# The cosine half of the index rotation moves behind TensorE's rotation, and its results are announced one by one

## The reference

```python
def rope(t):
    ...
    return jnp.concatenate([t1 * cos - t2 * sin, t1 * sin + t2 * cos], axis=-1)

p_rwkv, p_att, p_idx, p_gate = jnp.split(proj, c, axis=-1)
...
q_idx, k_idx, w_idx = jnp.split(p_idx, ci, axis=-1)
q_idx = rope(q_idx.reshape(B, S, IDX_HEADS, IDX_DIM))   # 8 heads of 64
k_idx = rope(k_idx[:, :, None, :])[:, :, 0, :]          # one key head of 64

# in the attention, for each block of 128 queries:
sc = jax.nn.relu(jnp.einsum('bqhd,bsd->bqhs', qib, k_idx))
score = jnp.einsum('bqhs,bqh->bqs', sc, wib) * idx_scale
_, sel = lax.top_k(score, topk)
```

## Time and profile before

| what | us |
|---|---|
| median of 3 runs | 2181.82 |
| lowest and highest run | 2179.98, 2184.24 |
| the profiled execution, its own time | 2179.98 |
| span of the profiled execution | 2178.2 |
| PE busy in the span | 2041.2 (94%) |
| PEld busy | 1637.1 (75%) |
| DVE busy | 926.5 (43%) |
| ACT busy | 804.3 (37%) |
| POOL busy | 984.4 (45%) |

### The profile page before, as it was taken

How to read it: one execution, slowest core, us unless ns; L and a number is a source line. 1 busy time by engine, 2 the same in 40 slices (tenths; PEclk the granted TensorE clock), 3 DMA queues, 4 the chain that set the end, 5 groups by cost and what they waited for, 6 DMA issues and landing times.

```text
span 2178.2 us, 26374 instructions
## 1 busy us (share of the span) xinstructions
PE 2041.2 (94%) x10214; PEld 1637.1 (75%) x10214; DVE 926.5 (43%) x1510; ACT 804.3 (37%) x1057; POOL 984.4 (45%) x766
## 2 busy tenths in 40 slices
PE   5997899999999998999999788999999899999998
PEld 3685797775777886888888576975886687888886
DVE  2579556666443134222200578347934452121101
ACT  3455224236555233222222453333225643222221
POOL 3535533545112454655466364003433255555663
PEclk9998999999999999999999899999999999999999
DMA  7211105521111231322222311001221222222222
GB/s 290 78 43 55 40 20 222 226 99 58 40 39 59 97 135 59 112 98 97 98 99 98 125 59 59 2 30 62 94 97 59 97 78 97 97 97 97 89 105 77
DMA packets 25898, 194.96 MB, mean 90 GB/s; under 512 B 3120, under 2 KB 3376, under 8 KB 4912
## 3 DMA queue, kind: packets, MB, share of 16 engines
q1 hardware_dynamic: 25776, 193.29, 24.4%
HBM read 189.09 MB, written 4.19 MB: 89 GB/s over the span
## 4 chain that ended last, share of the span: by engine, by line
PE 82%; DVE 8%; ACT 4%; POOL 2%; issue 2%; DMA 1%; SPq 0%; ACTq 0%; DVEq 0%; POOLq 0%
PE ps L399 22%; PE ps L401 22%; PE ps L400 22%; PE ps L467 2%; POOL W L2467 2%; ACT W L1272 1%; DMA ar<-ada_dram 1%; PE ps L497 1%; PE ps L837 1%; DVE ar L1831 1%; DVE ar L1857 1%; PE ps L892 1%; DVE ar L1809 1%; PE ps L824 1%; PE ps L601 1%
## 5 line engine op out<-in xcount | busy, mean ns | idle before, releaser
L2467 POOL TENSOR_TENSOR W<-raw,W 128x512 fp32r<-128x512 f32 x588 | 774.9, 1318 | 987.3 <-ACT W L1272 951.0
L399 PE MATMUL ps<-hH,W 128*128 128x512 f32 x1648 | 660.9, 401 | 46.0 <-DVE xL L1794 8.3
L401 PE MATMUL ps<-hH,W 128*128 128x512 f32 x1648 | 647.0, 393 | 0.0
L400 PE MATMUL ps<-arR,W 128*128 128x512 f32 x1392 | 542.8, 390 | 0.0
L1272 ACT CAST W<-raw 128x2048 fp32r<-128x2048 f32 x147 | 280.9, 1911 | 576.2 <-PE ps L401 551.2
L399 PEld LDWEIGHTS ps<-hH,W 128*128 128x128 f32 x1648 | 313.1, 190 | 130.7 <-issue 53.8
L401 PEld LDWEIGHTS ps<-hH,W 128*128 128x128 f32 x1648 | 312.6, 190 | 67.0
L400 PE MATMUL ps<-xL,W 128*128 128x512 f32 x848 | 335.4, 396 | 0.0
L400 PEld LDWEIGHTS ps<-arR,W 128*128 128x128 f32 x1392 | 262.1, 188 | 54.8 <-issue 0.2
L399 PE MATMUL ps<-arR,W 128*128 128x512 f32 x592 | 231.3, 391 | 3.3 <-DVE ar L1914 3.3
L401 PE MATMUL ps<-arR,W 128*128 128x512 f32 x592 | 231.1, 390 | 0.0
(11 more groups left out here) (384 smaller groups left out, 2264.9 us busy)
## 6 DMA issues: line engine op xcount, KB each, us to landing
raw<-panels_dram SPq DMA_DIRECT2D x147, 1024.0 KB, 4.8
ar<-ada_dram SPq DMA_DIRECT2D x12, 2048.0 KB, 11.4
xT<-xT_dram SPq DMA_DIRECT2D x2, 2048.0 KB, 9.0
out_dram<-xT SPq DMA_DIRECT2D x8, 512.0 KB, 2.6
xT<-out_dram SPq DMA_DIRECT2D x1, 2048.0 KB, 8.2
wide<-wide_dram SPq DMA_DIRECT2D x1, 1024.0 KB, 4.8
cm<-cm_dram SPq DMA_DIRECT2D x1, 832.0 KB, 30.6
ar<-lora_dram SPq DMA_DIRECT2D x1, 512.0 KB, 3.3
```

The source lines that it names most:

```text
L399: mm(out, lhs[0], rhs[0], start=first, stop=False)
L400: mm(out, lhs[0], rhs[1], start=False, stop=False)
L401: return mm(out, lhs[1], rhs[0], start=False, stop=final)
L2467: ins = tt(W[:, n % SPLIT, 1, c], raw[:, n % RAW, c], W[:, n % SPLIT, 0, c].bitcast(F32), ALU.subtract)
```

## The change

Five things change. (1) DVE no longer computes the five cosine products ahead of the rotation, and the five tiles for them are gone. (2) For each tile DVE now calls the helper `rope` with QI+i as source and destination and tile 39 as scratch: the sine product from PSUM into scratch (this one now frees the bank), the cosine product in place, and the sum. (3) Behind each tile DVE issues a one-column memset that raises the new semaphore `index_qk`. (4) PE makes the rotated partners in the order 0, 1, 2, 3, 4, while DVE still takes tile 4 first. (5) The index jobs of the first query block wait for `index_qk` to reach h // 2 + 2, that is for tile 4 and their own tile, where they waited for their tile's bank to be read.

```diff
-        INDEX_COS = 44
...
-                for i in (4, 0, 1, 2, 3):
+                for i in range(5):
                     emptied(pe, "ai", i)
                     begin("irot", i)
                     end(mm(pst("irot", i), const("rot"), tile(QI + i), start=True, stop=True))
...
-                        emptied(pe, "irot", h // 2)
+                        pe.wait_ge(sem("index_qk"), h // 2 + 2)
...
-                dve.wait_ge(trig_in, 16)
-                for i in range(5):
-                    emptied(dve, "ai", i)
-                    link(tt(tile(INDEX_COS + i), tile(QI + i), trig[:, 0, :], ALU.mult))
                 filled(dve, "wi_turn")
                 link(v.tensor_copy(sm2[:, WI:WI + 32], pst("wi_turn")[:, 0:32]), *read("wi_turn"))
+                dve.wait_ge(trig_in, 16)
                 for n, i in enumerate((4, 0, 1, 2, 3)):
-                    filled(dve, "irot", i)
-                    link(tt(pst("irot", i), pst("irot", i), trig[:, 1, :], ALU.mult))
-                    link(tt(tile(QI + i), pst("irot", i), tile(INDEX_COS + i), ALU.add), *read("irot", i))
+                    rope(tile(QI + i), tile(QI + i), "irot", i, tile(39))
+                    link(v.memset(st[:, 62:63], 0.0), sem("index_qk"), n + 1)
```

## The result

| | before | after |
|---|---|---|
| median, us | 2183.03 (4 runs, 2179.98 to 2184.87) | 2195.32 (4 runs, 2194.41 to 2196.35) |
| the profiled execution: span, own time | 2178.2, 2179.98 | 2189.8, 2191.66 |
| PE, DVE, POOL busy | 2041.2, 926.5, 984.4 | 2052.5, 924.2, 982.8 |

The change makes the kernel slower: the ratio is 1.0053, with a 95% interval of 1.0041 to 1.0065. The forecast was +7.0 us with a range up to 2193.0; it came out as +12.3 us between the medians and +11.6 us between the profiled executions. The record holds 21 executions of the changed kernel in all; they lie from 2189.88 to 2196.9 us with a median of 2194.41 and a mean of 2194.15, so the four are not at an extreme. The direction was right and the size too small, and the time lies above the range.

The account below looks back on a forecast made before the run. It took PE as busy 94% of the span, but waiting 7.30 us for DVE in the index part. +3.42 + 4.25 - 0.67 = +7.0 us on 2181.8 gave 2188.8 us, range 2184.5 to 2193.

Parts of the forecast that it names:

- The order of the partners: Index rotation: DVE takes tile 4 first but PE now makes it last, so DVE starts 3.42 us later.
- Three instructions and a memset for two: Index rotation on DVE: each of five tiles costs 2.31 us, together 11.55 instead of 7.30, plus 4.25 us.
- POOL's relief: Last "ai" panel: without DVE's cosine products beside them, two POOL pieces shorten, a gain of 0.67 us.
- The ring: Index jobs, relu and accumulations wait on each other, DVE slowest; "aq" starts a fixed 9.62 us after DVE's first accumulation.
- B (hidden): Slack between DVE and "aq" hides the index-part loss, leaving only POOL's 0.67 us gain: 2181.1 us; chance 0.05.
- C (partly absorbed): Index jobs run closer together, absorbing up to 3.7 us of PEld waits: +3.3 us, 2185.1 us; chance 0.06.
- Rival A, the clock: PE's gap in the index part halves the clock, possibly into "aq": at most +4.0 us, 2192.8 us; chance 0.08.
- the 10.2 us of the row: Half-clock time after an earlier 3.34 us PE gap, starting 4.4 us after PE stopped; used as pattern for the index part.
- Behind the index part: After the index part, all work shifts with "aq" by the same amount; nothing downstream gives the shift back.
- The width: Range of the forecast time, 2184.5 to 2193 us, using about 2 us of run spread either side of the median.

Follow-up runs that it names:

- e8: Kernel before with only PE's partner order changed to 0 to 4, DVE still taking tile 4 first; 2187.12 us, ratio 1.0013.
- e2: Changed kernel with one thing undone: PE again makes the partner of tile 4 first; 2188.08 us, ratio 1.0021 against the kernel before.
- e9: Changed kernel without the five memsets, the sum itself raising the new semaphore; 2191.19 us, ratio 1.0035 against the kernel before.
- e3: Changed kernel with ten extra, overwritten PE matmuls filling PE's idle time in the index part; 2193.43 us, ratio 1.0039 against the kernel before.
- e1: Changed kernel measured again, nothing altered; 2192.16 us, ratio 1.0041 against the kernel before.
- e6: Kernel before with three one-column memsets, 0.4 us of delay, between index rotation and first accumulation; 2185.19 us, ratio 1.0005.
- e7: Kernel before with partners made ahead of the narrow projection, two index jobs ahead of the turn, DVE rotating tile 4 last; 2180.12 us, ratio 0.9986.
- e4: Kernel before with extra, overwritten PE matmuls filling three 1.74 us waits in the sparse attention; 2182.23 us, ratio 0.9995.
- e0: Kernel before measured again, unchanged; 2184.13 us, ratio 1.0002.
- e5: Changed kernel with extra, overwritten PE matmuls filling three 1.74 us waits in the sparse attention; 2188.34 us, ratio 1.0025 against the kernel before.
- e10: Kernel before with the early rotation, cosine products delayed until the fourth ai tile is copied, and filled attention waits; 2181.79 us, ratio 0.9987.

## Why the prediction was wrong

**The order of the partners: right.** Summed 3.42 us, measured 3.44 (e8) and 3.43 (e2 against the changed kernel).

**Three instructions and a memset for two: right.** Summed 4.25 us, measured 4.24 (e2); one call 2.31 against 2.30. The memset's value of 0.13 us was 0.12 (e9).

**POOL's relief: right.** Summed 0.67; the gap fell by 0.67 us and the pieces from 1.63 to 1.30.

**The ring: right.** "aq" follows the first accumulation by 9.63 us, forecast 9.62, and the index part costs 7.67 - 0.67 = 7.0 us as forecast. The rivals B (hidden) and C (partly absorbed) did not occur.

**Rival A, the clock, in its place: right that it is free there.** The clock fell at 1497.3 us, 2.9 us after PE had stopped at 1494.36, where the prediction took 4.4 us from its row. The half clock lasted about 13.7 us (windows above: 2.7 + 5 + 5 + 1.0), longer than the 10.2 us of the row that I went by, and was over before "aq". With the clock kept up, nothing was gained (e3). The Trainium skill (TensorE: Matmul & The Clock Gate, What's actually happening) says that activity releases the throttled clock; the trace agrees, since it came back at 1511.0 us, when the index jobs ran close together.

**The step that failed: "Behind the index part".** There I wrote that everything behind shifts and "nothing gives the shift back", and took that as the whole truth about it: a shift by 7.0 us with no price of its own. The runs show that work behind the change can also become longer. In the sparse attention PE waits 1.74 us three times amid thin work, and whether the clock falls there goes with when it gets there. Of the profiles of kernels with the changed rotation and an attention as it was, the first paid nothing, and e1, e2, e3 and e9 paid 3.13, 3.13, 3.08 and 1.54 us. The two plain profiles of before and the order alone (e8) paid nothing, with 0.4 us of delay before paid 3.15 (e6), and the faster order paid 1.53 (e7). I had a row for the clock's fall and looked for its price only in the index part and in "aq". With 7.0 + 3.1 = 10.1 us the ratio would be 1.0046, which both measurements of the changed kernel hold (1.0041 to 1.0065, 1.0025 to 1.0057). 7.0 us alone, 1.0032, lies outside the first and inside the second. Between the medians it does not add up to all of it: the measured 2195.32 lies 6.5 us above the forecast 2188.8, of which 1.2 are the median of before (2183.03 beside 2181.82) and 3.1 at most the attention. The other 2 us or more stay open.

**The width: too small.** I took 2 us of spread from three runs. The 30 runs of before beside e4 to e7 lie from 2177.44 to 2185.97 us. The lag ahead of the index part alone ranged from 0 to 6.2 us in the table. The 4.7 us of it in the profiled pair are most likely not the change's doing, since before itself shows 4.16 in e0 and the changed kernel next to nothing in e1.

This is what is shown and what is only argued. The 7.0 us are shown part by part (e2, e8, e9). That the attention's price is the clock's is shown by e1 and e3 (falls with the loss) and by e5 (no waits, no fall, no loss there). That it is behind the difference of the medians is likely, not shown, because few executions of each kernel were profiled, and how often each kernel pays it stays open. The granted clock of every execution is on record and points the same way: it averages 0.9718 over the 21 executions of the changed kernel and 0.9772 over the 23 of before beside e0, which were measured at another time. My estimate from these means, (1 - clock) x 2 x span, is 123.6 and 99.4 us at half clock, 24 us more. The index part accounts for 13.7 of them, which were free, and two falls in the attention would for 6.8. So the time beyond 7.0 us goes with more half clock, partly also elsewhere. Why the outcome at the first wait sorts by the time since the clock's return stays open; e9 refuted the simple border.

## What to carry to other kernels

Where the chain of waits runs through an engine that is 43% busy, its work there costs in full: taking a product out of idle time and putting it behind the wait, and asking first for the operand that the other engine makes last, cost 4.25 and 3.42 us, and both could be read from before to a few hundredths. A delay is not only passed on: if there is work behind it in which TensorE waits again and again, as it does here for 1.74 us three times, the clock can fall there in one kernel and not in the other, so put both outcomes in the range. Before a difference of a few microseconds is explained from one pair of profiles, subtract the lag that exists ahead of the changed lines.

## What the hardware showed that I had not expected

- The clock fell behind waits of only 1.74 us (e1, e2, e3, e6, e7, e9) and 1.42 us (e10), where the shortest I had read from before was 3.34 us. In other executions the same waits were not followed by a fall, and two executions of the changed kernel with different outcomes stood 0.18 us apart, counted from the clock's return.
- A delay of 0.40 us was followed by 3.15 us of loss some 180 us later, among instructions that had not been changed (e6).
- Twelve machine matmuls that compute nothing, four in each of three waits, kept the clock at full speed there in both kernels (e4, e5).
